# Running the last down-projection pieces of a dense stage token block by token block

## The chip, the cores and the metric

The kernel runs on one core of a Trainium2 chip. The metric is the device time of one execution in microseconds (us); the median of three runs before the change is 1501.98 us.

The engines are named as the profile names them: PE is TensorE (matmuls), PEld its weight loads, DVE is VectorE, ACT is ScalarE, POOL is GpSimd, SP is the engine that issues most DMAs.

## The reference, cut to what matters

A sequence of 256 tokens with 1024 features goes through three blocks, all in float32. The parts that the change touches are matrix products that end in a 256 x 1024 result, which is then normed or added to the residual `h`:

```python
def sq_relu_mlp(h, w1, w2):
    a = jax.nn.relu(h @ w1)
    return (a * a) @ w2
...
    for i in range(DEPTH):                       # two layers
        pre = rms_norm(h, norm_g[i, 0])
        mix = s5_mixer(pre, ...) if i % 2 == 0 else dsa_mixer(pre, ...)   # both end in "... @ w_out"
        h = h + rms_norm(mix, norm_g[i, 1])
        ff = sq_relu_mlp(rms_norm(h, norm_g[i, 2]), mlp_w1[i], mlp_w2[i])
        h = h + rms_norm(ff, norm_g[i, 3])
...
    # second_block, at its end
        x = x + (jax.nn.silu(u_gate) * u_val) @ w_down[l]
    return x
```

`rms_norm` needs the sum of squares over all 1024 features of a token, but nothing of other tokens. So one half of the tokens can be normed while the other half is still being multiplied.

## The kernel before, in words

**Split numbers.** Every weight is cast into two parts, HI and LO, and every activation too (XH and XL, HH and HL, OH and OL). A product is three matmuls: high by HI, high by LO, low by HI.

**Pieces and the ring.** SP streams the weights in pieces through `raw`. ACT casts a piece to `HI` (L1246), DVE and POOL each subtract half of it to get `LO` (L443). HI and LO have four slots. The semaphores `lo_a` and `lo_b` tell PE that a piece is there (`arrived`), and PE tells with `piece_done` that it is through with one (`used`). Before ACT casts piece n it waits until piece n-4 is done. All queues are written out by hand, and each engine runs its own in order.

**A down-projection piece.** `down` multiplies one piece into `acc`, which holds 2 token blocks (tb, 128 tokens each) of 1024 outputs in PSUM. One piece holds `kt` (2, in the feed-forward stage 1) blocks of 128 rows of the weight. For each tb and each row block it issues 6 matmuls of 512 columns (3 products x 2 halves of the outputs), so 24 matmuls in a piece with kt=2, 12 with kt=1. The last piece of a stage raises `acc_first` after its tb 0; its `piece_done` tells that tb 1 is complete as well.

**The five stages of this case.** Their last pieces are: the S5 mixer's output product (2 pieces, 152.49 us to about 163.7 us), the last two pieces of the first MLP (from 345.22 us), the attention's output product (4 pieces, from 497.10 us), the last two pieces of the second MLP (from 700.49 us) and the last two pieces of the feed-forward stage of the second block (kt=1, from 1487.98 us). In the MLPs and the feed-forward stage a piece also waits for its hidden activations, `hid_lo` or `f_lo`, which ACT and DVE make from the up-projection just before.

**What comes after.** After the first four stages `post` runs:

- ACT takes the squares of `acc`, tb 0 (two instructions, L1262) once `acc_first` is up, then tb 1 once the last `piece_done` is up. Next on ACT stand the squares of the new `h` (`pre`), first those of tb 0.
- POOL makes 1/rms of each tb from them (L500, L501).
- DVE multiplies `acc` by the gain (`y`, L1769) and adds it into `h` (L1773), tb 0 and then tb 1; then it norms `h` for the next stage (L1751), PE transposes (L665), ACT and DVE split the result, and PE begins the next stage.

After the feed-forward stage DVE adds `acc` to `h` (L2374) per tb and half, and SP stores each half.

On ACT, in front of the squares of the attention's output product, stands `hi_to(P_ATT + 14)`, and on POOL and DVE the like calls: the casts of the next two pieces, P_ATT+13 and P_ATT+14, which belong to the second MLP. The output product has the pieces P_ATT+9 to P_ATT+12.

```python
            o1_high(N1 - 1)
            hi_to(P_ATT + 14)
            post(3, P_ATT + 12)
```

Of the kernel before, what the change touches and what calls it, by code (L numbers as in the profile page):

```python
# [14 lines left out]
P = 128  # L15
SEQ = 256
TB = SEQ // P
# [12 lines left out]
MC = DFF // 256  # L30
# [19 lines left out]
FC = DFF2 // P  # L50
# [66 lines left out]
def build(nc, ins, out):  # L117
    ctx = ExitStack()
    with ctx:
        def sb(name, shape, dt=F32):  # L120
            return ctx.enter_context(nc.sbuf_tensor(name, shape, dt))
# [3 lines left out]
        def S(name):  # L125
            if name not in sems:
                sems[name] = ctx.enter_context(nc.semaphore(name))
            return sems[name]
# [3 lines left out]
        HI = sb("HI", [P, 4, 2048], F32R)  # L132
        LO = sb("LO", [P, 4, 2048], F32R)
        XH = sb("XH", [P, KD, SEQ], F32R)
        XL = sb("XL", [P, KD, SEQ], F32R)
        HH = sb("HH", [P, 2, 2, SEQ], F32R)
        HL = sb("HL", [P, 2, 2, SEQ], F32R)
# [22 lines left out]
        acc = ctx.enter_context(nc.psum_tensor("acc", [P, TB, D], F32))  # L160
# [430 lines left out]
        def _(pe):  # L591
            ring = Ring()
            mm = nc.tensor.matmul

            def arrived():
                s, _, piece = ring.next()
                pe.wait_ge(S("lo_a"), piece + 1)
                pe.wait_ge(S("lo_b"), piece + 1)
                return s

            def used(ins):

                ins.then_inc(S("piece_done"), 1)
# [7 lines left out]
            def ch_major(s, bank, paired=False, norm=None):  # L611

                for j in range(2):
                    for k in range(KD):
                        w = (j * KD + k) * P if paired else k * 256 + j * P
                        if norm is not None and j == 0:
                            xT_wait(norm, 1, k)
                        last = three(wk[:, bank, j * SEQ:(j + 1) * SEQ], HI[:, s, w:w + P], LO[:, s, w:w + P],
                                     XH[:, k, :], XL[:, k, :], k == 0, k == KD - 1)
                return last  # L620
# [12 lines left out]
            def clear_acc():  # L633
                for q in range(4):
                    mm(accf[:, q * 512:(q + 1) * 512], zero_bf[:, 0:P], zero_bf[:, :], start=True, stop=False,
                       skip_group_check=True)

            def down(s, tiles, last_group, kt=2, first=False, norm=None):


                for tb in range(TB):
                    ts = slice(tb * P, (tb + 1) * P)
                    for kk in range(kt):
                        xh, xl = tiles(kk)
                        if norm is not None:
                            xT_wait(norm[0], tb, norm[1] + kk)
                        stop = last_group and kk == kt - 1
                        for lhs, w, begin, end in ((xh, HI, first and kk == 0, False), (xh, LO, False, False),
                                                   (xl, HI, False, stop)):
                            for n in range(2):  # L650
                                c = kk * 1024 + n * 512
                                last = mm(acc[:, tb, n * 512:(n + 1) * 512], lhs[:, ts], w[:, s, c:c + 512],  # L652
                                          start=begin, stop=end, skip_group_check=True)
                    if last_group and tb == 0:
                        last.then_inc(S("acc_first"), 1)
                return last

            def norm_transpose(n):

                for q in range(4):  # L660
                    tb, b = q // 2, q % 2
                    pe.wait_ge(S("y_ready"), 4 * n + q + 1)
                    for kk in range(4):
                        k = 4 * b + kk
                        last = nc.tensor.transpose(wk[:, q, kk * P:(kk + 1) * P], y[:, tb, k * P:(k + 1) * P], ident)  # L665
                    last.then_inc(S("xT_psum"), 1)

            def xT_wait(n, tb, k):

                if k % 4 == 0:  # L670
                    pe.wait_ge(S("xT_lo"), 4 * n + 2 * tb + k // 4 + 1)
# [14 lines left out]
            for b in range(2):  # L686
                s = arrived()
                last = ch_major(s, b, norm=0 if b == 0 else None)
# [3 lines left out]
            for r in range(2):  # L692
                for q in range(4):
                    last = nc.tensor.transpose(accf[:, 512 + r * 512 + q * P:512 + r * 512 + (q + 1) * P],
                                               cpad[:, r, q, :], ident)
# [4 lines left out]
            for r, n in enumerate(ROWS[1:]):  # L700
                last = nc.tensor.transpose(accf[:, 1536 + r * P:1536 + r * P + n], rows[0:n, 1 + r, :], ident[0:n, 0:n])
# [4 lines left out]
            for r in range(2):  # L706
                for q in range(4):
                    last = nc.tensor.transpose(wk[:, 2 + r, q * P:(q + 1) * P],
                                               bpad[:, r, 4 * q:4 * q + 4, :].rearrange("p a b -> p (a b)"), ident)
# [16 lines left out]
            def glu(s, k):  # L726

                pe.wait_ge(S("z_lo"), k + 1)
                for b in range(2):
                    for j in range(2):  # L730
                        w = k * 512 + (2 * b + j) * P
                        last = three(wk[:, b, j * SEQ:(j + 1) * SEQ], HI[:, s, w:w + P], LO[:, s, w:w + P],
                                     XH[:, k, :], XL[:, k, :], False, k == 3, True)
                    if k == 3 and b == 0:
                        last.then_inc(S("glu_psum"), 1)
                return last
# [3 lines left out]
            for i in range(ST):  # L740
# [6 lines left out]
                for n, (c, x) in enumerate(((ct5[:, 0, q, js], prod_re[:, b, 0, :]), (ct5n[:, q, js], prod_re[:, b, 1, :]),  # L747
                                            (ct5[:, 1, q, js], prod_im[:, b, 0, :]), (ct5[:, 1, q, js], prod_im[:, b, 1, :]))):
                    last = mm(accf[js, q * 512:q * 512 + SEQ], c, x, start=(n == 0), stop=(n == 3))
# [9 lines left out]
                if i >= 13:  # L759
                    last = glu(glu_slot, i - 13)  # L760
            last = glu(glu_slot, 3)
            used(last)
            pe.wait_ge(S("z2_lo"), 2)
            for p in range(2):
                s = arrived()
                used(down(s, lambda kk: (XH[:, 4 + 2 * p + kk, :], XL[:, 4 + 2 * p + kk, :]), p == 1, first=p == 0))

            def mlp(layer):

                norm_transpose(1 + 2 * layer)  # L770
                base = layer * MC

                def mlp_up(c, par):

                    if not (isinstance(c, int) and c + base < 2):
                        pe.wait_ge(S("hid_read"), c + base - 1)
                    s = arrived()
                    used(ch_major(s, par, norm=1 + 2 * layer if isinstance(c, int) and c == 0 else None))

                def mlp_down(c, par, end=False):  # L780
                    pe.wait_ge(S("hid_lo"), c + base + 1)
                    s = arrived()
                    used(down(s, lambda kk: (HH[:, par, kk, :], HL[:, par, kk, :]), end))

                def turn(c):
                    mlp_up(c + 1, 1)
                    mlp_down(c, 0)
                    mlp_up(c + 2, 0)
                    mlp_down(c + 1, 1)

                mlp_up(0, 0)
                clear_acc()
                turn(0)
                with pe.Fori(0, MC // 2 - 2) as i:
                    ring.enter(i, 1)
                    turn(i * 2 + 2)
                ring.leave(MC // 2 - 2)
                mlp_up(MC - 1, 1)
                mlp_down(MC - 2, 0)
                mlp_down(MC - 1, 1, True)  # L800

            mlp(0)


            norm_transpose(2)

            def proj1(e, part):
# [34 lines left out]
            s = arrived()  # L842
# [80 lines left out]
                if n >= 1:  # L923
                    weighted1(n - 1)
            pe.wait_ge(S("o1_lo"), len(JOBS1))
            for p in range(4):
                s = arrived()
                used(down(s, lambda kk: (XH[:, 2 * p + kk, :], XL[:, 2 * p + kk, :]), p == 3, first=p == 0))

            mlp(1)  # L930


# [17 lines left out]
            for c in range(9):  # L950
# [9 lines left out]
                for part in range(2):  # L960
                    s = arrived()
                    used(tok_major(s, lambda tb: wk[:, bank2(c) + tb, :], 4 * part, 4, 512, part == 0, part == 1,
                                   norm=4 if c == 0 else None))
                if c == 0:
                    s = arrived()
# [6 lines left out]
            for n, (lhs, b) in enumerate(((UU, 0), (UU, 1), (GT, 0))):  # L972
                last = mm(accf[:, 1024 + n * 32:1024 + (n + 1) * 32], lhs, a_tok[:, b, :], start=True, stop=True)
# [77 lines left out]
            for p in range(2):  # L1051
                s = arrived()
# [125 lines left out]
            for p in range(4):  # L1178
                s = arrived()
# [12 lines left out]
            def ffn_down(c, par, end=False):  # L1192
                pe.wait_ge(S("f_lo"), c + 1)
                s = arrived()
                used(down(s, lambda kk: (HH[:, par, kk, :], HL[:, par, kk, :]), end, kt=1))
# [12 lines left out]
                ffn_turn(i * 2 + 2)  # L1208
            ring.leave(FC // 2 - 2)
            ffn_up(FC - 1, 1)  # L1210
            ffn_down(FC - 2, 0)
            ffn_down(FC - 1, 1, True)

# [1254 lines left out]
```

## Time and profile before

| what | value |
|---|---|
| three runs | 1501.98, 1500.94, 1505.4 us |
| median | 1501.98 us |
| span of the profiled execution | 1502.7 us (no other time of that execution is listed) |
| PE matmul busy | 1318.7 us, 88% of the span |
| DVE busy | 977.8 us, 65% |
| ACT busy | 634.5 us, 42% |
| POOL busy | 589.4 us, 39% |
| matmuls of `down` (L652) | 1512 in all, by the groups of the trace |

The three runs lie 4.5 us apart. The busy shares are averages over stages with different limits; what counts for this change is the few microseconds around the end of each of the five stages.

### The profile page before, as it was taken

How to read it: one execution, taken by the hardware profiler on the slowest of the kernel's cores; microseconds unless marked ns; L12 is line 12 of the kernel's file. 1: busy time of each engine (PE TensorE's matmuls, PEld its weight loads, DVE VectorE, ACT ScalarE, POOL GpSimd, SP SyncE). 2: the span in 40 equal slices, each digit the busy share in tenths (PEclk: the TensorE clock that was granted, in tenths of full speed). 3: DMA queues.
4: the chain of work that ended last, by engine and by line, in shares of the span. 5: the costliest groups of instructions: out<-in, count | busy, mean ns of one | idle time of the engine just before them, and what ended most of it. 6: DMA issues, size and time to landing. Idle time of an engine off the chain costs nothing.

```text
span 1502.7 us, 21949 instructions
## 1 busy us (share of the span) xinstructions
PE 1318.7 (88%) x7938; PEld 1130.8 (75%) x7943; DVE 977.8 (65%) x1528; ACT 634.5 (42%) x1045; POOL 589.4 (39%) x367
## 2 busy tenths in 40 slices
PE   3378799998979799999999999999899768888887
PEld 2234699997856699998788888888888657877775
DVE  7998533334774543333655666589999975788787
ACT  4301444444434554444354544355444423434433
POOL 6498444444530444443343322233332212334332
PEclk8688899999977999999799999999999979999999
DMA  7000565664300566564375423444334303354553
GB/s 230 1 29 30 179 184 183 193 182 150 111 29 1 168 195 193 174 194 142 98 229 165 138 86 87 123 142 126 112 112 140 140 28 113 113 165 149 151 164 98
DMA packets 170401, 197.04 MB, mean 131 GB/s; under 512 B 14049, under 2 KB 135397, under 8 KB 170341
## 3 DMA queue, kind: packets, MB, share of 16 engines
q1 hardware_dynamic: 169115, 192.03, 42.0%
q10 hardware_dynamic: 1226, 4.21, 0.8%
q8 instruction: 37, 0.61, 0.2%
q14 instruction: 23, 0.19, 0.0%
HBM read 195.17 MB, written 1.05 MB: 131 GB/s over the span
## 4 chain that ended last, share of the span: by engine, by line
PE 55%; DVE 28%; issue 7%; ACT 6%; POOL 4%; DMA 0%; ACTq 0%; DVEq 0%; POOLq 0%
PE acc L652 17%; PE wk L607 9%; PE wk L608 9%; PE wk L609 9%; DVE fp L2335 3%; DVE arena L2342 3%; ACT HI L1246 3%; DVE LO L443 2%; DVE arena L2237 2%; PE wk L884 2%; DVE arena L2185 1%; DVE arena L2221 1%; PE acc L607 1%; DVE arena L2249 1%; PE wk L1005 1%
## 5 line engine op out<-in xcount | busy, mean ns | idle before, releaser
L443 POOL TENSOR_TENSOR LO<-raw,HI 128x1024 fp32r<-128x1024 f32 (+3 forms) x191 | 455.5, 2386 | 824.2 <-ACT HI L1246 823.9
L1246 ACT ACTIVATE HI<-raw 128x1024 fp32r<-128x1024 f32 (+3 forms) x382 | 359.8, 993 | 154.8 <-PE acc L652 70.5
L607 PE MATMUL wk<-XH,HI 128*128 128x256 f32 x1296 | 376.6, 291 | 31.8 <-POOL LO L443 19.7
L608 PE MATMUL wk<-XL,HI 128*128 128x256 f32 x1296 | 371.4, 287 | 0.0
L609 PE MATMUL wk<-XH,LO 128*128 128x256 f32 x1296 | 370.9, 286 | 0.0
L443 DVE TENSOR_TENSOR LO<-raw,HI 128x1024 fp32r<-128x1024 f32 (+3 forms) x191 | 243.5, 1277 | 185.8 <-ACT HI L1246 183.6
L607 PEld LDWEIGHTS wk<-XH,HI 128*128 128x128 f32 x1296 | 253.3, 195 | 46.2 <-issue 42.9
L608 PEld LDWEIGHTS wk<-XL,HI 128*128 128x128 f32 x1296 | 253.5, 196 | 1.3
L609 PEld LDWEIGHTS wk<-XH,LO 128*128 128x128 f32 x1296 | 253.3, 195 | 0.0
L652 PE MATMUL acc<-HI,HH 128*128 128x512 f32 x424 | 135.1, 400 | 35.8 <-POOL LO L443 17.6
L652 PE MATMUL acc<-LO,HH 128*128 128x512 f32 x424 | 132.3, 393 | 0.0
L652 PE MATMUL acc<-HI,HL 128*128 128x512 f32 x424 | 132.2, 393 | 0.0
L652 PEld LDWEIGHTS acc<-HI,HH 128*128 128x128 f32 x424 | 76.3, 191 | 53.7 <-issue 31.3
L1941 DVE TENSOR_TENSOR arena<-arena 128x512 f32<-128x512 f32 x32 | 22.2, 693 | 127.3 <-ACT arena L1374 127.3
L607 PE MATMUL wk<-HI,XH 128*128 128x512 f32 (+2 forms) x240 | 95.7, 399 | 6.6 <-DVE LO L443 5.7
L608 PE MATMUL wk<-LO,XH 128*128 128x512 f32 (+2 forms) x240 | 94.0, 392 | 0.0
L609 PE MATMUL wk<-HI,XL 128*128 128x512 f32 (+2 forms) x240 | 93.7, 391 | 0.0
L652 PEld LDWEIGHTS acc<-LO,HH 128*128 128x128 f32 x424 | 80.5, 190 | 17.5
L652 PEld LDWEIGHTS acc<-HI,HL 128*128 128x128 f32 x424 | 80.5, 190 | 17.3
L1374 ACT ACTIVATE arena<-wk 128x512 f32<-128x512 f32 x32 | 19.2, 599 | 119.8 <-PE wk L609 119.8
L607 PEld LDWEIGHTS wk<-HI,XH 128*128 128x128 f32 x240 | 49.0, 204 | 16.1 <-DVE LO L443 6.2
L609 PEld LDWEIGHTS wk<-HI,XL 128*128 128x128 f32 x240 | 48.8, 203 | 9.0
(318 smaller groups left out, 2021.9 us busy)
## 6 DMA issues: line engine op xcount, KB each, us to landing
raw<-in_mlp_w SPq DMA_DIRECT2D x128, 512.0 KB, 4.2
raw<-in_w_in SPq DMA_DIRECT2D x100, 512.0 KB, 4.0
raw<-in_w_up SPq DMA_DIRECT2D x44, 512.0 KB, 4.5
raw<-in_w_down SPq DMA_DIRECT2D x44, 256.0 KB, 2.9
raw<-in_att_w_in SPq DMA_DIRECT2D x16, 512.0 KB, 4.1
raw<-in_w_ssd_proj SPq DMA_DIRECT2D x16, 512.0 KB, 3.6
raw<-in_att_w_out SPq DMA_DIRECT2D x8, 512.0 KB, 4.0
raw<-in_w_out SPq DMA_DIRECT2D x8, 512.0 KB, 3.4
```

The source lines that it names most:

```text
L443: tensor_tensor(LO[:, s, cs], raw[:, s % 2, "ab".index(part), 0:m], HI[:, s, cs].bitcast(F32), ALU.subtract).then_inc(S(f"lo_{part}"), 1)
L607: mm(o, lh, rh, start=start, stop=False, skip_group_check=skip)
L608: mm(o, lh, rl, start=False, stop=False, skip_group_check=skip)
L609: return mm(o, ll, rh, start=False, stop=stop, skip_group_check=skip)
L652: last = mm(acc[:, tb, n * 512:(n + 1) * 512], lhs[:, ts], w[:, s, c:c + 512], start=begin, stop=end, skip_group_check=True)
L884: last = mm(o, qT1[hs, hd // 2, tb * P:(tb + 1) * P], kT1[hs, hd // 4, 0:K], start=False, stop=True, skip_group_check=True)
L1246: A(HI[:, s, j * m:(j + 1) * m], raw[:, s % 2, j, 0:m], ACT.Copy).then_inc(S(f"hi_{part}"), 1)
L1374: A(relu_b[:, par, :], wk[:, par, :], ACT.Relu).then_inc(S("hid_read"), 1)
L1941: link(TT(sq_b[:, par, :], relu_b[:, par, :], relu_b[:, par, :], ALU.mult))
L2237: TT(Lm[:, m, :], Lm[:, m, :], cbs[:, :], ALU.mult).then_inc(S("M_ready"), 1)
L2335: V.tensor_copy(fp[:, par, :], fpall[:, bass.ds(c, 1), :].rearrange("p a n -> p (a n)"))\
L2342: last = TS(o, s, w[0], w[3], ALU.mult, ALU.add) if k == 0 else STT(o, s, w[k], o, ALU.mult, ALU.add)
```

## The change

A new function `last_downs` takes several pieces at once. Its outer loop runs over the token blocks, its inner one over the pieces: tb 0 of all pieces, then `acc_first`, then tb 1 of all pieces. A piece is waited for in the tb 0 pass and marked as used in the tb 1 pass. The wait for the hidden activations of a piece stands in front of its tb 0 part. The number of matmuls, their operands and their shapes stay what they were.

```diff
+            def last_downs(tiles, ready=(), kt=2, first=False):
+                slots = []
+                for tb in range(TB):
+                    ts = slice(tb * P, (tb + 1) * P)
+                    for p in range(len(tiles)):
+                        if tb == 0:
+                            if ready:
+                                pe.wait_ge(*ready[p])
+                            slots.append(arrived())
+                        for kk in range(kt):
+                            xh, xl = tiles[p](kk)
+                            end = p == len(tiles) - 1 and kk == kt - 1
+                            for lhs, w, begin, stop in ((xh, HI, first and p == 0 and kk == 0, False), (xh, LO, False, False),
+                                                        (xl, HI, False, end)):
+                                for n in range(2):
+                                    c = kk * 1024 + n * 512
+                                    last = mm(acc[:, tb, n * 512:(n + 1) * 512], lhs[:, ts], w[:, slots[p], c:c + 512],
+                                              start=begin, stop=stop, skip_group_check=True)
+                        if tb == 1:
+                            used(last)
+                    if tb == 0:
+                        last.then_inc(S("acc_first"), 1)
...
-            for p in range(2):
-                s = arrived()
-                used(down(s, lambda kk: (XH[:, 4 + 2 * p + kk, :], XL[:, 4 + 2 * p + kk, :]), p == 1, first=p == 0))
+            last_downs([lambda kk, p=p: (XH[:, 4 + 2 * p + kk, :], XL[:, 4 + 2 * p + kk, :]) for p in range(2)], first=True)
...
-                mlp_down(MC - 2, 0)
-                mlp_down(MC - 1, 1, True)
+                last_downs([lambda kk, par=par: (HH[:, par, kk, :], HL[:, par, kk, :]) for par in range(2)],
+                           [(S("hid_lo"), MC - 1 + base), (S("hid_lo"), MC + base)])
...
-            for p in range(4):
-                s = arrived()
-                used(down(s, lambda kk: (XH[:, 2 * p + kk, :], XL[:, 2 * p + kk, :]), p == 3, first=p == 0))
+            last_downs([lambda kk, p=p: (XH[:, 2 * p + kk, :], XL[:, 2 * p + kk, :]) for p in range(4)], first=True)
...
-            ffn_down(FC - 2, 0)
-            ffn_down(FC - 1, 1, True)
+            last_downs([lambda kk, par=par: (HH[:, par, kk, :], HL[:, par, kk, :]) for par in range(2)],
+                       [(S("f_lo"), FC - 1), (S("f_lo"), FC)], kt=1)
```

The first place is PE's queue at the end of the feed-forward stage, the last two pieces; a row is line, operation, output<-inputs, columns and count, and the semaphores that it waits for. Before:

```order
L652 MATMUL acc<-HI,HH 128x512 [waits lo_b,lo_a,f_lo]
L652 MATMUL acc<-HI,HH 128x512
L652 MATMUL acc<-LO,HH 128x512 x2
L652 MATMUL acc<-HI,HL 128x512 x2
L652 MATMUL acc<-HI,HH 128x512 x2
L652 MATMUL acc<-LO,HH 128x512 x2
L652 MATMUL acc<-HI,HL 128x512 x2
L652 MATMUL acc<-HI,HH 128x512 [waits lo_b,lo_a,f_lo]
L652 MATMUL acc<-HI,HH 128x512
L652 MATMUL acc<-LO,HH 128x512 x2
L652 MATMUL acc<-HI,HL 128x512 x2
```

The same place of PE's queue in the changed kernel, down to its last matmul but six:

```order
L675 MATMUL acc<-HI,HH 128x512 [waits lo_b,lo_a,f_lo]
L675 MATMUL acc<-HI,HH 128x512
L675 MATMUL acc<-LO,HH 128x512 x2
L675 MATMUL acc<-HI,HL 128x512 x2
L675 MATMUL acc<-HI,HH 128x512 [waits lo_b,lo_a,f_lo]
L675 MATMUL acc<-HI,HH 128x512
L675 MATMUL acc<-LO,HH 128x512 x2
L675 MATMUL acc<-HI,HL 128x512 x2
L675 MATMUL acc<-HI,HH 128x512 x2
L675 MATMUL acc<-LO,HH 128x512 x2
L675 MATMUL acc<-HI,HL 128x512 x2
```

The wait for the last hidden activations (the second `f_lo`) stood behind 12 matmuls and in front of 12; it stands now behind 6 and in front of 18.

The second place is PE's queue in the attention's output product, from the middle of its first piece on. Before:

```order
L652 MATMUL acc<-HI,XH 128x512 x2
L652 MATMUL acc<-LO,XH 128x512 x2
L652 MATMUL acc<-HI,XL 128x512 x2
L652 MATMUL acc<-HI,XH 128x512 x2
L652 MATMUL acc<-LO,XH 128x512 x2
L652 MATMUL acc<-HI,XL 128x512 x2
L652 MATMUL acc<-HI,XH 128x512 [waits lo_b,lo_a]
L652 MATMUL acc<-HI,XH 128x512
```

In the changed kernel, from the start of the stage on (`o1_lo` is the wait for its input):

```order
L675 MATMUL acc<-HI,XH 128x512 [waits lo_b,lo_a,o1_lo]
L675 MATMUL acc<-HI,XH 128x512
L675 MATMUL acc<-LO,XH 128x512 x2
L675 MATMUL acc<-HI,XL 128x512 x2
L675 MATMUL acc<-HI,XH 128x512 x2
L675 MATMUL acc<-LO,XH 128x512 x2
L675 MATMUL acc<-HI,XL 128x512 x2
L675 MATMUL acc<-HI,XH 128x512 [waits lo_b,lo_a]
L675 MATMUL acc<-HI,XH 128x512
```

The second piece was waited for after 24 matmuls and is waited for after 12 now; the same holds for the third and the fourth.

## Rows read from the trace of the kernel before

**Rows 1.** The page: its head, and busy times with shares of the span.

```profile
span 1502.7 us, 21949 instructions
...
PE 1318.7 (88%) x7938; PEld 1130.8 (75%) x7943; DVE 977.8 (65%) x1528; ACT 634.5 (42%) x1045; POOL 589.4 (39%) x367
```

**Rows 2.** The page: the chain that ended last, by engine.

```profile
PE 55%; DVE 28%; issue 7%; ACT 6%; POOL 4%; DMA 0%; ACTq 0%; DVEq 0%; POOLq 0%
```

**Rows 3.** The chain, S5 output product: start us, us, what.

```profile
152.49 8.47 PE acc L652 x36
...
163.41 1.42 DVE h L1773 x2
...
166.10 0.76 DVE h L1773
```

**Rows 4.** The chain, end of the first MLP.

```profile
345.22 10.92 PE acc L652 x48
```

**Rows 5.** Timeline of ACT, first MLP's end: start us, us, engine, line, operation.

```profile
353.44 0.60 ACT L1262 ACTIVATE arena<-acc 128x512 f32<-128x512 f32 x1 [5.03 <-PE acc L652]
...
356.16 0.60 ACT L1262 ACTIVATE arena<-acc 128x512 f32<-128x512 f32 x1 [1.45 <-PE acc L652]
...
357.32 0.63 ACT L1262 ACTIVATE arena<-h 128x512 f32<-128x512 f32 x1
```

**Rows 6.** Timeline of DVE, the same stretch.

```profile
346.62 0.69 DVE L1943 TENSOR_TENSOR HL<-arena,HH 128x512 fp32r<-128x512 f32 x1
...
357.19 1.28 DVE L1769 TENSOR_TENSOR y<-acc,gpost 128x512 f32<-128x512 f32 x2
358.56 1.42 DVE L1773 SCALAR_TENSOR_TENSOR h<-y,rstd,h 128x512 f32<-128x512 f32 x2
```

**Rows 7.** Timeline of POOL, the same stretch.

```profile
357.53 0.30 POOL L500 TENSOR_SCALAR nv<-ssq 128x1 f32<-128x1 f32 x1 [1.77 <-ACT arena L1262]
357.90 0.56 POOL L501 TENSOR_TENSOR rstd<-nv,half 128x1 f32<-128x1 f32 x1
```

**Rows 8.** The chain, the attention's output product.

```profile
497.10 19.37 PE acc L652 x84
```

**Rows 9.** Timeline of ACT, the attention's output product.

```profile
508.33 2.01 ACT L1246 ACTIVATE HI<-raw 128x1024 fp32r<-128x1024 f32 x2 [1.88 <-PE acc L652]
516.49 0.60 ACT L1262 ACTIVATE arena<-acc 128x512 f32<-128x512 f32 x1 [6.15 <-PE acc L652]
```

**Rows 10.** Timeline of POOL, the same stretch.

```profile
501.16 3.38 POOL L443 TENSOR_TENSOR LO<-raw,HI 128x1024 fp32r<-128x1024 f32 x1
...
510.42 2.48 POOL L443 TENSOR_TENSOR LO<-raw,HI 128x1024 fp32r<-128x1024 f32 x1 [1.50 <-ACT HI L1246]
```

**Rows 11.** Timeline of PE, the feed-forward stage's last two pieces.

```profile
1487.98 0.70 PE L652 MATMUL acc<-HI,HH 128*128 128x512 f32 x2 [0.88 <-POOL LO L443]
...
1490.35 0.61 PE L652 MATMUL acc<-HI,HL 128*128 128x512 f32 x2
1494.50 0.73 PE L652 MATMUL acc<-HI,HH 128*128 128x512 f32 x2 [3.53 <-DVE HL L2350]
```

**Rows 12.** Timeline of DVE, the same stretch.

```profile
1494.02 0.43 DVE L2350 TENSOR_TENSOR HL<-arena,HH 128x256 fp32r<-128x256 f32 x1 [0.48 <-ACT HH L1692]
...
1498.88 1.28 DVE L2374 TENSOR_TENSOR y<-h,acc 128x512 f32<-128x512 f32 x2 [1.27 <-PE acc L652]
```

**Rows 13.** The chain, the last piece of the feed-forward stage.

```profile
1494.50 4.36 PE acc L652 x12
```

**Rows 14.** PE in half microseconds: stretch, length, busy (count), granted clock, DMA.

```profile
1495.50:1496.00 0.50, 0.50 (x3) 0.87 0.00 0
1496.00:1496.50 0.50, 0.50 (x2) 0.50 0.00 0
...
1498.50:1499.00 0.50, 0.34 (x1) 0.50 1.03 385
...
1499.50:1500.00 0.50, 0.00 (x0) 1.00 0.00 0
```

## The prediction

> **What bounds the kernel now.** I read the page first. The span is 1502.7 us and PE is busy for 88% of it [rows 1]; the chain that ended last spends 55% of the span on PE and 28% on DVE [rows 2]. So the kernel is neither all matmul nor all waiting, and the average says nothing about the ends of five stages. For these I read the chain and the timelines of ACT, DVE and POOL around each end, and ask one question: does anything after the stage wait for token block 0, or only for token block 1?
>
> At first sight the chain says block 0. In the S5 output product it leaves PE after 36 of the 48 matmuls, just when `acc_first` goes up, and enters DVE's `h` of block 0 at 163.41 [rows 3]. In the attention's product it leaves PE after 84 of 96 [rows 8]. A reader who stops here expects a gain: `acc_first` comes 12 matmuls earlier with two pieces and 36 earlier with four. But at the end of the first MLP the chain runs through all 48 matmuls [rows 4]. The chain names only the release that came last, and a tie of hundredths decides which.
>
> The timelines of the first MLP's end show the tie. PE ends block 1 at 345.22 + 10.92 = 356.14 [rows 4]. From there: ACT takes the squares of block 1 at 356.16 and, without any gap, those of the new `h` of block 0 at 357.32 [rows 5]. So `h` of block 0 was already there, and ACT was held only by its own queue behind block 1. POOL starts its part for block 1 at 357.53 and ends at 357.90 + 0.56 = 358.46 [rows 7]. DVE, late with block 0, starts `y` of block 1 at 357.19 and ends at 358.47, and starts `h` of block 1 at 358.56 [rows 6]. DVE being free (358.47) and POOL's result (358.46) meet within 0.01 us. In the S5 stage block 1 ends 12 matmuls after 160.96, at 163.7, and `h` of block 1 starts at 166.10 [rows 3], 2.4 us later, as here (358.56 - 356.14 = 2.42). The other two ends repeat this spacing. So four ends hang on the end of block 1, which has the same matmuls in front of it as before.
>
> **The change part by part.**
>
> Matmuls. None is added or removed. 48 take 10.92 us [rows 4], 0.2275 us each; the reordered ones have the same shapes. Cost 0.
>
> Earlier `acc_first` (S5, both MLPs). It comes 12 x 0.2275 = 2.73 us earlier, and with it squares, 1/rms and `h` of block 0. DVE is then idle when the squares of block 1 come. `y` of block 1 can start some 0.3 us earlier, but `h` of block 1 still waits for POOL until 358.46 plus the same 0.10 us. ACT's queue is full from 356.16 on anyway [rows 5]. Gain 0.0 to 0.02 us at each end. The most it could be, if POOL's two instructions also became shorter because DVE is quieter, is the 0.3 us by which DVE was late. I take 0.
>
> The wait for the hidden activations in the MLPs. Before, 24 matmuls (5.46 us) cover it; now 12 cover 2.73 us, until 345.22 + 2.73 = 347.95. The last HL is written at 346.62 + 0.69 = 347.31 [rows 6]. It is covered by 0.64 us. Were the cover gone, PE would lose what is missing, and everything behind it. Cost 0, above 0.64 us of lateness one for one.
>
> The attention's product, weights. Block 0 wants a piece every 2.73 us, not every 5.46. The fourth is wanted at 497.10 + 0.25 (84 matmuls took 19.37 us, 0.26 more than at 0.2275 each [rows 8]) + 3 x 2.73 = 505.5. POOL ends its LO at 501.16 + 3.38 = 504.54 [rows 10]. Covered by 1.0 us. Cost 0.
>
> The attention's product, what is queued in front of the squares. This is where the change takes something back. ACT must cast the next two pieces before the squares of block 0, and these wait for the first and second piece to be done. Before, that was after 24 and 48 matmuls (the second pair of casts starts at 508.33 [rows 9]). Now it is after 60 and 72: about 511.0 and 513.7. The casts take 2.01 us, so they end at 515.7. ACT's squares of block 0 then run from 515.7, earlier than 516.49 [rows 9]. But POOL's LO of the second one stands in front of its 1/rms: 515.8 + 2.48 = 518.3 [rows 10], then 0.37 + 0.56 for the 1/rms [rows 7]: 519.2, `h` of block 0 from 519.3 to 520.7, `y` of block 1 to 522.0, `h` of block 1 at 522.1. By the spacing of the other ends it started at 516.49 - 0.02 + 2.73 + 2.42 = 521.6. So the end comes 0.3 to 0.5 us later; with POOL's longest cast, 3.38 in place of 2.48, 1.4; with none of the overlaps as I draw them, 0. I take +0.4. The loads that wait for these casts land long before ACT turns to them, since the norm of the next stage lies between.
>
> The feed-forward stage. Here the wait is not covered. PE does 12 matmuls from 1487.98, is done about 1490.8, and idles 3.53 us until HL of the last hidden block is there, 1494.02 + 0.43 [rows 11, 12]. Then 12 more take 4.36 us [rows 13], and the end of the program hangs on them: DVE's last adds start at 1498.88 [rows 12]. In the new order only 6 matmuls lie before the wait and 18 behind it. The 6 that slid behind the wait are pure loss for block 1; block 0 is complete after the same 6 as before. At the full clock 6 cost 6 x 0.2275 = 1.37 us. But the granted clock is falling in the middle of this piece, from 1.00 (2.4 GHz) to 0.50 (1.2 GHz) between 1495.5 and 1496.0, still 0.50 at 1498.9, and back at 1.00 from 1499.5 [rows 14]. At half clock a matmul takes twice 512 columns at 2.4 GHz, 0.427 us, and 6 cost 2.56. The idle hole in front of it grows from 3.5 to 4.9 us, which can make the fall come earlier. Were all 18 at half clock, they would take 7.7 us, 3.3 more than the 4.36 now. Were the clock low from the first on and back at 1499.25 (between those two rows), 4.75 us would hold 11.1 slow ones, and 6.9 fast ones would follow in 1.57: 6.3 us, 2.0 more. The ends are +1.4 and +3.3; I take +2.3, near their middle.
>
> A rule speaks to this hole. The Trainium skill, "TensorE: Matmul & The Clock Gate", section "Why this matters for your kernels", warns that idle gaps between matmul bursts drop the engine back to half rate, and Part 1 adds that the moment isn't tied to the kernel, so that it can shift from run to run. By that rule the longer hole costs the full +3.3 us; if one went only by the six extra matmuls it would be +1.4. The trace agrees as far as it goes: the fall stands behind the hole of 3.53 us [rows 11, 14].
>
> Sum, against the profiled span: 1502.7 + 0 (four stages' `acc_first`) + 0.4 + 2.3 = 1505.4 us. That span is 0.7 us above the median of the runs, 1501.98; so the forecast time is 1501.98 + 2.7 = 1504.7 us.
>
> **The rivals.**
>
> A, the earlier block 0 pays. If the chain is right and what follows hangs on `acc_first`, each of the S5 and MLP ends gains 2.7 us, and the attention's as much or more: 4 x 2.7 = 10.9 less, 2.3 back at the end: 1493.4. For it: the chain leaves PE at `acc_first` twice [rows 3, 8]. Against it: ACT's squares of block 1 follow PE's end by 0.02 us and leave no gap behind them [rows 5].
>
> B, slower. In the attention's product PE stalls for the fourth piece because pieces are wanted at twice the pace. It decides from 1.0 us of lateness on; one POOL cast of 3.38 us more in front of it costs 2.4 us, and the total is 1507.1. For it: that row shows casts stretching from 2.48 to 3.38 us [rows 10]. Against it: the casts that come between now start later, so they disturb less.
>
> C, a small gain at each end. POOL becomes quicker with DVE idle: 4 x 0.3 = 1.2 us, total 1503.5. Nothing shows it: POOL's 0.30 and 0.56 already stand beside a light DVE load [rows 6, 7].
>
> **How the numbers follow.** Each has a chance: forecast 0.76, A 0.04, B 0.10, C 0.10. A measurement of this kernel can tell about 0.3%, 4.5 us, from no change; the three runs lie as far apart. The forecast and C are within it, apart from the scatter of the runs; B is just over. Faster by over 0.3%: A and a little scatter, 0.06. Slower: B and the upper end of the forecast (the attention's +1.4 and the last stage's +3.3 together are 4.7), 0.16. Within: 0.78. The range is 1501.5 to 1507.5: below, the least at the end (+1.4), C's gain (-1.2) and a scatter of 0.7; above, B. A is left out.
>
> **What would show it.** In the profile after, at the four ends: ACT's squares of block 0 2.7 us earlier, those of block 1 still 0.02 us behind PE's end, `h` of block 1 still 2.4 us behind it. In the attention's product: casts at about 511 and 513.7, POOL's cast directly in front of its 1/rms. At the end: PE idle about 4.9 us behind six matmuls, then 18 in one go, the last at 1.4 to 3.3 us more than before; block 0's adds before or at their old time. I am wrong if PE idles in the MLP between its two parts, or if `h` of block 1 comes nearer to PE's end.

## The result, and the profile after

The changed kernel takes 1507.64 us (median of 20 runs, 1502.66 to 1509.24). The kernel before, run beside it, takes 1504.96 us (median of 20, 1500.5 to 1507.26). The ratio is 1.0021 with a 95% interval of 1.0013 to 1.0028, so the change costs 3.2 us (2.0 to 4.2). The forecast was +2.7 us. The forecast time, 1504.7, was built on the median of the three runs shown, 1501.98, which lies 3.0 us below that of the twenty; so the measured time lies 0.14 us above the range.

The page's head and its busy times of the changed kernel:

```profile
span 1507.0 us, 21949 instructions
...
PE 1320.2 (88%) x7938; PEld 1131.0 (75%) x7943; DVE 980.8 (65%) x1528; ACT 634.5 (42%) x1045; POOL 589.6 (39%) x367
```

The span is 4.35 us longer than in [rows 1], with the same instructions and nearly the same busy time (PE 1.5 us more): most of what changed is waiting.

**The end of the first MLP.** The timeline of ACT after the change (start us, us, engine, line, operation; in brackets the idle time before):

```profile
352.81 0.60 ACT L1282 ACTIVATE arena<-acc 128x512 f32<-128x512 f32 x1 [2.31 <-PE acc L675]
...
358.25 0.60 ACT L1282 ACTIVATE arena<-acc 128x512 f32<-128x512 f32 x1 [4.17 <-PE acc L675]
...
359.41 0.63 ACT L1282 ACTIVATE arena<-h 128x512 f32<-128x512 f32 x1
```

Against [rows 5] block 0's squares lead block 1's by 5.44 us and not 2.72. But the squares of the new `h` of block 0 still stand directly behind block 1's, 1.16 us after them, as before (357.32 - 356.16). The lead ends in ACT's queue: its idle time in front of block 1 grew from 1.45 to 4.17 us. DVE in the same stretch:

```profile
355.23 1.42 DVE L1793 SCALAR_TENSOR_TENSOR h<-y,rstd,h 128x512 f32<-128x512 f32 x2 [0.33 <-POOL rstd L501]
358.97 1.29 DVE L1789 TENSOR_TENSOR y<-acc,gpost 128x512 f32<-128x512 f32 x2 [2.33 <-ACT arena L1282]
360.65 1.42 DVE L1793 SCALAR_TENSOR_TENSOR h<-y,rstd,h 128x512 f32<-128x512 f32 x2 [0.39 <-POOL rstd L501]
```

`y` of block 1 starts 0.72 us after the squares (1.03 before, [rows 5, 6]), so DVE's lateness is gone, and `h` of block 1 starts 2.40 us after them, as before. DVE now waits 0.39 us for POOL instead.

What the end of a stage costs is read first as the time from the squares of block 1 to the first matmul of the next stage. PE's first matmul of the attention's projection in the kernel before, and then in the changed one:

```profile
364.80 0.78 PE L607 MATMUL wk<-HI,XH 128*128 128x512 f32 x1
```

```profile
366.89 0.78 PE L607 MATMUL wk<-HI,XH 128*128 128x512 f32 x1
```

364.80 - 356.16 and 366.89 - 358.25 are both 8.64 us. I use this distance in the table of the experiments. It says when the next stage starts, not how fast that stage then runs; for the attention's product this makes a difference (below).

**The attention's output product.** The chain through it, which ran through 84 matmuls and straight into the squares before [rows 8]:

```profile
499.09 16.63 PE acc L675 x72
...
517.82 3.12 POOL LO L443
...
522.09 1.42 DVE h L1793 x2
```

It leaves PE after 72 matmuls now, when the second piece is released, and goes through a cast and POOL's LO. ACT's timeline shows the queue:

```profile
513.02 2.01 ACT L1266 ACTIVATE HI<-raw 128x1024 fp32r<-128x1024 f32 x2 [10.02 <-PE acc L675]
515.74 2.01 ACT L1266 ACTIVATE HI<-raw 128x1024 fp32r<-128x1024 f32 x2 [0.71 <-PE acc L675]
517.77 0.60 ACT L1282 ACTIVATE arena<-acc 128x512 f32<-128x512 f32 x1
```

Block 0 of `acc` was complete at about 510.3 (499.09 + 0.25 + 48 x 0.2275), and its squares start at 517.77: 7.5 us of the lead are spent waiting and casting. The next matmul of PE starts here:

```profile
531.74 0.55 PE L607 MATMUL wk<-XH,HI 128*128 128x256 f32 x1 [0.65 <-DVE XL L1780]
```

Block 1's squares started at 521.18, so the distance is 10.56 us; before it was 528.84 - 519.21 = 9.63:

```profile
519.21 0.60 ACT L1262 ACTIVATE arena<-acc 128x512 f32<-128x512 f32 x1 [1.45 <-PE acc L652]
...
528.84 0.55 PE L607 MATMUL wk<-XH,HI 128*128 128x256 f32 x1 [0.65 <-DVE XL L1760]
```

The next stage starts 0.93 us later. But not all of this is lost. The next stage begins at the low clock, and the low stretch of PE's clock is shorter by five matmuls in the changed kernel. Before, and then after (stretch, length, busy, granted clock, DMA):

```profile
528.85:533.30 4.45, 4.45 (x21) 0.50 0.80 260
```

```profile
531.75:535.20 3.45, 3.45 (x16) 0.50 0.83 287
```

In both profiles the clock is back at 1.00 some 14 us behind PE's last matmul of the attention's product (519.19 and 521.16), so the later start lets fewer matmuls fall into the low stretch. The chain at the first down-projection piece of the second MLP, before and then after, shows what is left:

```profile
543.41 5.47 PE acc L652 x24
```

```profile
545.89 5.47 PE acc L652 x24
```

From block 1's squares it is 24.20 us before and 24.71 after. The stage costs 0.93 us at its end and 0.5 us net.

**The end of the feed-forward stage.** PE's timeline and the chain:

```profile
1496.69 1.22 PE L675 MATMUL acc<-HI,HH 128*128 128x512 f32 x2 [4.89 <-DVE HL L2370]
```

```profile
1496.69 6.52 PE acc L675 x18
```

The hole is 4.89 us and not 3.53; its end is set by DVE's HL, so the growth alone costs nothing. Behind it 6.52 us of matmuls follow and not 4.36 [rows 11, 13]: 2.16 us more. The stretches of PE's clock (stretch, length, busy, granted clock, DMA):

```profile
1496.00:1499.50 3.50, 2.81 (x7) 0.50 0.00 0
...
1501.00:1501.50 0.50, 0.50 (x3) 0.77 0.55 209
1501.50:1503.50 2.00, 1.70 (x8) 1.00 0.57 210
```

The clock stands at 0.50 (1.2 GHz) from the first matmul on, where before it fell in the middle of the piece [rows 14], and is back at 1.00 for the last eight.

### The profile page after: what moved, and what is told of

It reads as the page before. It is cut to its first block, busy times and chain, and to the rows that moved or that the text cites. A ratio compares the mean times of both kernels' runs of the same rounds, so it can differ in the third digit from the quotient of the medians.

```text
span 1507.0 us, 21949 instructions
## 1 busy us (share of the span) xinstructions
PE 1320.2 (88%) x7938; PEld 1131.0 (75%) x7943; DVE 980.8 (65%) x1528; ACT 634.5 (42%) x1045; POOL 589.6 (39%) x367
## 4 chain that ended last, share of the span: by engine, by line
PE 55%; DVE 27%; issue 6%; ACT 6%; POOL 4%; DMA 1%; ACTq 0%; DVEq 0%; SPq 0%; POOLq 0%
PE acc L652 13%; PE wk L607 9%; PE wk L609 8%; PE wk L608 8%; PE acc L675 4%; DVE fp L2355 3%; ACT HI L1266 3%; DVE arena L2362 3%; DVE LO L443 2%; PE wk L906 2%; DVE arena L2257 1%; DVE arena L2205 1%; PE acc L607 1%; DVE arena L2241 1%; PE wk L1025 1%
## 5 line engine op out<-in xcount | busy, mean ns | idle before, releaser
L652 PE MATMUL acc<-HI,HH 128*128 128x512 f32 x384 | 121.9, 399 | 31.0 <-POOL LO L443 16.6
L652 PE MATMUL acc<-LO,HH 128*128 128x512 f32 x384 | 119.6, 393 | 0.0
L652 PE MATMUL acc<-HI,HL 128*128 128x512 f32 x384 | 119.2, 392 | 0.0
L1961 DVE TENSOR_TENSOR arena<-arena 128x512 f32<-128x512 f32 x32 | 22.2, 693 | 126.8 <-ACT arena L1394 126.8
L652 PEld LDWEIGHTS acc<-HI,HH 128*128 128x128 f32 x384 | 68.7, 190 | 47.4 <-issue 30.9
L652 PEld LDWEIGHTS acc<-LO,HH 128*128 128x128 f32 x384 | 72.7, 189 | 15.8
L652 PEld LDWEIGHTS acc<-HI,HL 128*128 128x128 f32 x384 | 72.7, 189 | 15.7
```

The lines of the kernel that those rows point to most:

```text
L1961: link(TT(sq_b[:, par, :], relu_b[:, par, :], relu_b[:, par, :], ALU.mult))
```

## The experiments

All are compared with the kernel before, run on the same chip in five rounds each (6 to 12 runs of the kernel). The diffs are cuts against the changed kernel, in e6 against e5. "Old order" is `down` piece by piece, "new order" is `last_downs`.

**e1: new order in the S5 output product and both MLPs only.**

```diff
-            last_downs([lambda kk, p=p: (XH[:, 2 * p + kk, :], XL[:, 2 * p + kk, :]) for p in range(4)], first=True)
+            for p in range(4):
+                s = arrived()
+                used(down(s, lambda kk: (XH[:, 2 * p + kk, :], XL[:, 2 * p + kk, :]), p == 3, first=p == 0))
...
-            last_downs([lambda kk, par=par: (HH[:, par, kk, :], HL[:, par, kk, :]) for par in range(2)],
-                       [(S("f_lo"), FC - 1), (S("f_lo"), FC)], kt=1)
+            ffn_down(FC - 2, 0)
+            ffn_down(FC - 1, 1, True)
```

> New order in the S5 output product and at the ends of both MLPs only; attention's product and feed-forward stage as before. Theory (all hangs on block 1): the earlier acc_first buys nothing and the reorder costs nothing, ratio to before 1.000 (0.0 us, within 0.5); in the profile h of block 1 starts 2.42 us after PE's last matmul, as in both kernels. Rival 1 (the earlier block 0 pays at each end and the other two places hide it): 0.3 to 2.7 us less at each of three ends, 1 to 8 us faster. Rival 2 (the half clock that the changed kernel's profile shows in the S5 product belongs to the new order): +1.5 us, and the dip there again.

Measured: ratio 1.0004 (0.9992 to 1.0017). The distances at the three ends are 9.64, 8.64 and 8.64 us, those of the kernel before to a hundredth. A gain of 2.7 us at each end (8 in all) is outside the interval, and a gain of 0.3 at each is excluded by the distances. The half clock needs a look. In the profile of the changed kernel the S5 product took 12.68 us, in this one 13.82, against some 11.2 before (the chains, first the changed kernel, then e1):

```profile
153.21 12.68 PE acc L675 x48
```

```profile
151.87 13.82 PE acc L675 x48
```

But e3, which has the old order there, shows it too (36 matmuls, 8.47 us in [rows 3]), and e4, which has the new order, does not:

```profile
153.04 10.07 PE acc L652 x36
```

```profile
152.41 11.23 PE acc L677 x48
```

So the dip neither needs the new order nor always comes with it, and rival 2 falls as it was put. Whether the new order makes the dip more likely stays open: it is in three of the four profiles with the new order there, and in two of the five with the old one. In e1 and e3 most or all of it also came back. From block 1's squares to the first down-projection piece of the MLP it is 22.25 us in both, against 24.44 in the kernel before, since there the next stage started at full clock: 2.2 us back for a dip of 2.6 us in e1 and of 1.6 in e3. In the changed kernel's profile it is 24.32, and the dip is paid.

**e2: new order in the attention's output product only.** The edit is e1's turned round: the S5, MLP and feed-forward calls are put back.

```diff
-                last_downs([lambda kk, par=par: (HH[:, par, kk, :], HL[:, par, kk, :]) for par in range(2)],
-                           [(S("hid_lo"), MC - 1 + base), (S("hid_lo"), MC + base)])
+                mlp_down(MC - 2, 0)
+                mlp_down(MC - 1, 1, True)
```

> New order in the attention's output product only (4 pieces). Theory (casts queued in front of the squares of block 0 and POOL's 1/rms come later, because the first two pieces are released later): +0.9 us (0.6 to 1.2), ratio 1.0006; h of block 1 starts about 3.5 us after PE's last matmul and not 2.4. Rival (PE waits for the third or fourth piece): an idle stretch of PE inside the product, its 96 matmuls taking over 22.1 us. Rival of no cost: 0, h of block 1 at 2.4 us.

Measured: ratio 1.0006 (0.9994 to 1.0018), which by itself tells nothing from zero. The distance does: 529.60 - 519.05 = 10.55 us against 9.63, and `h` of block 1 starts 3.6 us behind PE's end, as the theory said. To the first down-projection piece of the MLP it is 24.72 us against 24.20, so 0.5 us of the 0.9 are net. POOL's timeline in it:

```profile
515.70 3.12 POOL L443 TENSOR_TENSOR LO<-raw,HI 128x1024 fp32r<-128x1024 f32 x1 [0.23 <-ACT HI L1268]
518.91 0.29 POOL L500 TENSOR_SCALAR nv<-ssq 128x1 f32<-128x1 f32 x1
```

POOL begins block 0's 1/rms 0.09 us after its cast. PE went through the 96 matmuls in 22.09 us by the distance 496.95 to 519.04, with no wait for a piece.

**e3: new order in the feed-forward stage only.** The edit puts back the other three calls.

```diff
-            last_downs([lambda kk, p=p: (XH[:, 4 + 2 * p + kk, :], XL[:, 4 + 2 * p + kk, :]) for p in range(2)], first=True)
+            for p in range(2):
+                s = arrived()
+                used(down(s, lambda kk: (XH[:, 4 + 2 * p + kk, :], XL[:, 4 + 2 * p + kk, :]), p == 1, first=p == 0))
```

> New order in the last two pieces of the feed-forward stage only. Theory (six matmuls slide behind an uncovered wait): +2.2 us (1.4 to 3.3, by where the granted clock stands), ratio 1.0015; PE idle 4.9 us and then 18 matmuls in 5.5 to 7.7 us. Rival (the loss in the changed kernel is the shifted clock, not the six matmuls): under 1 us.

Measured: ratio 1.0010 (0.9995 to 1.0025), which includes both no change and the 2.2 us expected. In the profile the hole and the 18 matmuls repeat those of the changed kernel:

```profile
1494.04 1.22 PE L675 MATMUL acc<-HI,HH 128*128 128x512 f32 x2 [4.89 <-DVE HL L2374]
```

The last stretch of PE takes 6.56 us, 2.20 more than the 4.36 before. Six matmuls at full clock are 1.37 us of it; the other 0.8 are the lower clock. So the rival, under 1 us and the clock alone, falls.

**e4: new order in four stages, and block 0 ahead of the casts in the attention's.** The same callback stands in POOL's `row_rstd` and DVE's `post`.

```diff
-            hi_to(P_ATT + 14)
-            post(3, P_ATT + 12)
+            hi_to(P_ATT + 12)
+            post(3, P_ATT + 12, lambda: hi_to(P_ATT + 14))
...
                 for tb, (sem, count) in enumerate((("acc_first", n), ("piece_done", last_piece + 1))):
+                    if tb == 1 and between is not None:
+                        between()
```

> New order at the S5, MLP and attention ends, feed-forward stage as before, and in the attention's product ACT, DVE and POOL do block 0's squares, 1/rms and h ahead of the casts of the next two pieces. Theory: the attention's +0.9 us goes away and nothing is gained in its place, ratio 1.000 (within 0.5 us); h of block 1 again 2.4 us after PE's last matmul. Rival (the cost is not the queue but the later release of the ring): +0.9 us stays.

Measured: ratio 0.9994 (0.9981 to 1.0008). ACT in the attention's product:

```profile
508.02 0.60 ACT L1284 ACTIVATE arena<-acc 128x512 f32<-128x512 f32 x1 [7.49 <-PE acc L677]
...
518.90 0.60 ACT L1284 ACTIVATE arena<-acc 128x512 f32<-128x512 f32 x1 [3.43 <-PE acc L677]
```

Block 0's squares lead block 1's by 10.9 us, and the distance is 528.53 - 518.90 = 9.63 us again. The 0.93 us are gone, though the pieces are released just as late as in e2 (ACT's first cast of the pair starts 13.9 us after the product in both). So the cost was the queue, and even 10.9 us of lead buy nothing. One more thing in this profile: its last piece of the feed-forward stage, in the old order, ran wholly at full clock behind a hole of 3.55 us (the chain, and PE's clock in that stretch),

```profile
1490.47 3.07 PE acc L654 x12
```

```profile
1490.40:1493.60 3.20, 3.06 (x12) 1.00 0.00 0
```

against 4.36 in [rows 13], 4.53 in e1 and 4.41 in e2. The same 12 matmuls differ by up to 1.46 us.

**e5: like e4, and the norm goes block by block.** The loops over the blocks of `post` and `pre` are merged on ACT, POOL (`pair_rstd`) and DVE; on DVE the second half of block 0's norm stays behind `h` of block 1. In the attention's product one cast pair stands behind block 0's squares of `acc`, the other behind those of `h`.

```diff
-            def post(n, last_piece):
+            def both(n, last_piece, a=None, b=None):
                 for tb, (sem, count) in enumerate((("acc_first", n), ("piece_done", last_piece + 1))):
-                    for n in range(2):
-                        squares(acc, tb, n, sem, count)
+                    for u in range(2):
+                        squares(acc, tb, u, sem, count)
+                    if tb == 0 and a is not None:
+                        a()
+                    for u in range(2):
+                        squares(h, tb, u, "h_ready", 2 * (TB * (n - 1) + tb) + u + 1)
+                    if tb == 0 and b is not None:
+                        b()
```

> New order at the S5, MLP and attention ends (feed-forward stage as before), and the norm behind them goes block by block: ACT takes the squares of the new h of block 0 and POOL its 1/rms before those of acc's block 1, DVE norms the first half of block 0 in its idle time before block 1. Theory (the early acc_first is worth nothing only because ACT's queue holds block 0's next step behind block 1): now it is worth something, the time from PE's last matmul of the stage to its first of the next falls from 9.6 and 8.6 us to about 8.8 and 7.9, 3 to 4 us in all, ratio 0.998. Rival (block 1's own chain of squares, 1/rms, h and squares sets everything): that time stays as it was, ratio 1.000.

Measured: ratio 0.9994 (0.9981 to 1.0007). The distances fall, by less than expected: 9.07, 8.07, 9.39 and 8.07 us against 9.64, 8.64, 9.63 and 8.64, in sum 1.95 us. ACT at the first MLP's end:

```profile
354.35 0.63 ACT L1290 ACTIVATE arena<-h 128x512 f32<-128x512 f32 x1 [1.93 <-DVE h L1808]
...
356.59 0.60 ACT L1290 ACTIVATE arena<-acc 128x512 f32<-128x512 f32 x1 [0.85 <-PE acc L683]
...
359.79 0.63 ACT L1290 ACTIVATE arena<-h 128x512 f32<-128x512 f32 x1 [1.93 <-DVE h L1808]
```

Block 0's squares of `h` are through before block 1's of `acc` begin. What is left is block 1's own chain: its squares of `h` start 3.20 us after those of `acc` (3.19 in the kernel before), and no lead of block 0 shortens that part.

**e6: the same norm block by block, with the old order everywhere.** The edit is e5's norm; all calls of `last_downs` are put back. One of the three places in which it differs from e5:

```diff
-                last_downs([lambda kk, par=par: (HH[:, par, kk, :], HL[:, par, kk, :]) for par in range(2)],
-                           [(S("hid_lo"), MC - 1 + base), (S("hid_lo"), MC + base)])
+                mlp_down(MC - 2, 0)
+                mlp_down(MC - 1, 1, True)
```

> The same norm block by block, with the old order of the matmuls everywhere (acc_first only 12 matmuls, 2.7 us, before the end). Theory (what the reorder buys is the lead of block 0): h of block 0 is ready only 0.4 us after PE's end, so its squares stand in front of block 1's and push them by some 1.7 us; the time to the next stage rises to about 10.4 and 9.4 us, 3 us slower than before in all, ratio 1.002. Rival (the order of the norm alone brings what e5 brings): like e5.

Measured: ratio 1.0096 (1.0078 to 1.0114), 14.5 us slower (11.7 to 17.2); the sign was right, the size far off. ACT at the first MLP's end:

```profile
358.17 0.60 ACT L1294 ACTIVATE arena<-acc 128x512 f32<-128x512 f32 x1 [5.03 <-PE acc L660]
...
361.37 0.63 ACT L1294 ACTIVATE arena<-h 128x512 f32<-128x512 f32 x1 [1.93 <-DVE h L1812]
...
362.67 0.58 ACT L1294 ACTIVATE arena<-acc 128x512 f32<-128x512 f32 x1
```

PE ended block 1 12 matmuls after 358.15, at 360.88; its squares start at 362.67, behind those of `h` of block 0. From PE's end to the next stage it is 10.65 us there, 2.0 more than before, and 2.0 more at the S5 and the second MLP's end: near the 1.7 expected. The rest is the attention's product, which I had not worked out: 17.1 us from PE's end to the next stage, 7.5 more. There both pairs of casts fall behind PE's late `acc_first`, with POOL and DVE in each other's way (below). The sum of the four, 13.5 us, lies inside the measured interval. The profile does not add up so simply: its S5 product was 2.9 us longer (36 matmuls in 11.35 us, the half clock again), and from the first MLP's last pieces to the attention's product it took 1.0 us less than before (150.88 against 151.88), though the attention's stage started 2.0 us later behind PE's end. Why is open.

**e7: feed-forward stage only, with all 24 matmuls behind the wait.**

```diff
-                       [(S("f_lo"), FC - 1), (S("f_lo"), FC)], kt=1)
+                       [(S("f_lo"), FC), (S("f_lo"), FC)], kt=1)
```

> New order in the feed-forward stage only, and also the first of the two pieces waits for the last hidden activations, so that all 24 matmuls stand behind the uncovered wait. Theory (each matmul that slides behind it is lost): PE's last stretch has 24 matmuls and takes 1.4 to 2.6 us more than the 6.5 us of 18, 3.6 us or more over the kernel before, ratio 1.0025. Rival (the loss is a fixed price of a longer hole, not a price per matmul): as e3, 2.2 us.

Measured: ratio 1.0019 (1.0007 to 1.0031), 2.9 us slower (1.1 to 4.7). That holds the 3.6 us expected and the rival's 2.2 as well; the profile tells them apart. PE's timeline and the chain:

```profile
1494.80 1.22 PE L675 MATMUL acc<-HI,HH 128*128 128x512 f32 x2 [7.35 <-DVE HL L2374]
```

```profile
1494.80 7.98 PE acc L675 x24
```

12, 18 and 24 matmuls behind the wait take 4.36, 6.56 and 7.98 us. The third six cost 1.42, full clock (6 x 0.2275 = 1.37), the second 2.20. So each matmul behind the wait is paid for, at the clock that it meets, and the rival of a fixed price falls.

The readings side by side: distance from block 1's squares to the next stage's first matmul (for e6 from PE's end, which is 0.02 us earlier), and PE's last stretch.

```
kernel    S5     MLP 1  attention  MLP 2  last stretch of PE    ratio (95%)
before    9.64   8.64   9.63       8.64   12 matmuls, 4.36      1
changed   9.64   8.64   10.56      8.64   18 matmuls, 6.52      1.0021 (1.0013-1.0028)
e1        9.64   8.64   9.64       8.64   12 matmuls, 4.53      1.0004 (0.9992-1.0017)
e2        9.63   8.63   10.55      8.63   12 matmuls, 4.41      1.0006 (0.9994-1.0018)
e3        9.64   8.63   9.64       8.64   18 matmuls, 6.56      1.0010 (0.9995-1.0025)
e4        9.63   8.63   9.63       8.63   12 matmuls, 3.07      0.9994 (0.9981-1.0008)
e5        9.07   8.07   9.39       8.07   12 matmuls, 4.41      0.9994 (0.9981-1.0007)
e6        11.66  10.65  17.10      10.64  12 matmuls, 4.40      1.0096 (1.0078-1.0114)
e7        9.64   8.64   9.64       8.64   24 matmuls, 7.98      1.0019 (1.0007-1.0031)
```

## Why the prediction was right or wrong

**What failed: the starting point of the sum, and with it the range.** The step was "that span is 0.7 us above the median of the runs, 1501.98; so the forecast time is 1501.98 + 2.7". Two things are wrong in it. The three runs lay 4.5 us apart, and the median of twenty is 1504.96, 3.0 us higher; of all triples that can be drawn from the twenty, about one in seven has a median as low as 1501.98. And a span was compared with device times. The device time is 1.9 us longer than the span in the changed kernel's profiled execution (1508.91 against 1507.0), and 1.8 to 1.9 in the other runs. By that, the span of 1502.7 stood for some 1504.6 us, 2.6 above the median of three, and 1504.6 + 2.7 would have been 1507.3. The range did not make up for it: it allowed 0.7 us of scatter at its lower end and 0.4 above rival B's 1507.1 at its upper end, where its starting point was uncertain by some 3 us both ways. The mechanism was not what failed.

**The four ends: right.** The step "four ends hang on the end of block 1" held: three distances are unchanged to a hundredth of a microsecond, in the changed kernel and in e1. Rival A, that the earlier block 0 pays, is refuted by e1 and e4. Rival C, a small gain from a quieter POOL, did not show: at the first MLP's end POOL's two instructions still take 0.30 and 0.56 us, though DVE is idle in front of them. The point on which the chain misleads, a tie of hundredths between two releases, is confirmed by the profile after, in which it runs through all 48 matmuls of the S5 product.

**The wait for the hidden activations in the MLPs: right.** PE's 48 matmuls take 10.92 us at the second MLP's end after the change, as before.

**The attention's product: right place, and the size right only net.** The term "I take +0.4" measured 0.93 us at the start of the next stage (0.92 in e2), inside its bounds of 0 and 1.4, and 0.5 net. The queue was as drawn: squares of block 0 behind the casts, then `y` of block 1 behind `h` of block 0. What was too small was POOL's second cast, put at 2.48 us; it took 3.12. That is most of the 0.8 us by which `h` of block 0 came later than drawn (23.0 us behind the product's start and not 22.2). That the next stage pays 0.43 us back at the low clock was not in the working, so the net agreement is partly luck. e4 shows the cause: with block 0 ahead of the casts the cost is gone. Rival B, a stall of PE for the fourth piece, did not come.

**The feed-forward stage: right.** Forecast +2.3, measured 2.16 us in the profile and 2.20 in e3. The hole of 4.9 us and the low clock from the first of the 18 matmuls were as described. The upper bound of +3.3, all 18 at half clock, did not come, since the clock was back before the last eight. The rule of the Trainium skill ("TensorE: Matmul & The Clock Gate", "Why this matters for your kernels"), that idle gaps between bursts drop the clock to half, agrees with the trace here and in e3 and e7, where the clock fell inside the hole. In e4 it does not show: the 12 matmuls behind a hole of 3.55 us ran at 1.00. Against e4's 3.07 us the same change would have cost 3.5, an estimate (6.52 - 3.07).

**The sum.** 0.5 + 2.16 = 2.7 us from the profile (3.1 with the attention's 0.93), 3.2 (2.0 to 4.2) measured. The spans differ by 4.35 us. Of the other 1.7, PE starts the S5 product 0.72 us later (153.21 against 152.49), which no part of the change touches, and that product takes 1.5 us longer at its half clock, which e3 shows in the old order as well; the stages between win some 0.5 back.

**What stays open.** Whether e5 beats the kernel before: in its profile the next stages start 1.95 us earlier in sum; the interval of its ratio, -2.9 to +1.1 us, does not decide. Why the clock dips in some profiles' S5 product, and why e4's last piece met none, no run shows. No run took away the MLPs' 0.64 us of cover.

## What to carry to other kernels

To start one half of a result earlier is worth something only if the half that comes last has a shorter way behind it. Follow the last half from its release to the next stage first, and then ask, queue by queue, whether the early half's next step stands behind the late half's. Each matmul that a reordering puts behind a wait which nothing covers is paid in full, and a reordering that moves a buffer's release later is paid where the next user of the buffer stands in some queue, not where the buffer is.

Read a late start at a later mark too: the stage that started 0.93 us late was 0.5 us late at its first down-projection piece, since less of it fell into the low clock.

A time forecast built on three runs carries their scatter, and a span is not a device time. The difference can be forecast closer than the time.

## What the runs showed of the hardware

The granted clock moved the same work by more than the change's single terms: the same 12 matmuls took 3.07 to 4.53 us, and the 48 of the S5 product from 11.2 to 14.1 us (in e6, 36 in 11.35 and 12 more), between profiles whose instructions there are the same or only reordered. In the changed kernel's profile the S5 product began at half clock:

```profile
153.00:156.00 3.00, 2.79 (x7) 0.50 1.05 396
```

POOL and DVE slow each other down when both cast. In e6's attention product POOL's LO cast, DVE's LO cast and POOL's 1/rms step on one number per partition followed each other like this:

```profile
523.44 2.80 POOL L443 TENSOR_TENSOR LO<-raw,HI 128x1024 fp32r<-128x1024 f32 x1 [0.93 <-ACT HI L1278]
...
526.34 1.15 POOL L512 TENSOR_SCALAR nv<-ssq 128x1 f32<-128x1 f32 x1
```

```profile
523.95 3.38 DVE L443 TENSOR_TENSOR LO<-raw,HI 128x1024 fp32r<-128x1024 f32 x1
```

DVE's cast takes 1.23 us alone. Here it takes 3.38 and ends at 527.33, 1.09 us after POOL's cast is through (526.24). POOL's next instruction, 0.30 us in [rows 7], takes 1.15 and ends just behind DVE's cast. The Trainium skill, "SBUF — State Buffer", section "SBUF: two separate sides", says that the port pair shared by VectorE and GpSimd is locked for a whole instruction, for a VectorE instruction with two inputs in SBUF only against one of GpSimd that reads SBUF, and that the other is blocked until it ends. These rows agree with it.

The same would explain POOL's cast of 3.12 us in the changed kernel's attention product, the part of the attention's term that was mis-sized. POOL's first cast of the pair, and DVE's second one:

```profile
515.11 2.49 POOL L443 TENSOR_TENSOR LO<-raw,HI 128x1024 fp32r<-128x1024 f32 x1 [8.59 <-ACT HI L1266]
```

```profile
516.83 1.85 DVE L443 TENSOR_TENSOR LO<-raw,HI 128x1024 fp32r<-128x1024 f32 x1 [1.50 <-ACT HI L1266]
```

DVE's cast starts beside POOL's first and ends at 518.68, 1.08 us behind its end. POOL's second cast starts at 517.82 beside DVE's and ends at 520.94, 2.26 us behind that one's end. No run took DVE's cast away, so the cause is read from the order of the rows and not shown by an experiment.
